# RWKV scan run as two streams half an iteration apart, with three projection groups ahead of the loop

## What is computed

```
n = rmsnorm(h); z = n @ w_in_2            # columns: b, c, h (conv), r, k, v (scan), low ranks
y_conv = b * causal_conv3(c * h)
r, k, v = token_shift(...)                # lerp with the previous position
S_t = S_{t-1} diag(w_t) + (S_{t-1} a_t) b_t^T + v_t k_t^T ;  y_t = S_t r_t      # 16 heads of 64
y = group_norm(y) * ln_x_w + ln_x_b + bonus ; y_rwkv = y * gate
h = h + rmsnorm([y_conv, y_rwkv] @ w_out_2) ; then the feed-forward part
```

## Time and profile before

| | |
|---|---|
| median of 3 runs | 2535.88 us (2532.89 to 2537.92) |
| the profiled execution, its own time | 2540.15 us |
| its span, first to last instruction | 2538.4 us |
| PE busy over the span | 2488.8 us (98%) |
| DVE, ACT, POOL busy | 1660.2, 1209.3, 71.4 us |
| the scan loop (first row of `k1` to first row of `out2`) | 1240.86 to 1670.29 us of the span |

### The profile page before, as it was taken

The page is one execution under the profiler, slowest core; times in us unless marked ns, Lnnn a source line. Parts: engine busy times, 40 slices in busy tenths (PEclk is TensorE's granted clock), DMA queues, the critical chain, the costliest instruction groups (busy, mean ns, idle before and its releaser), DMA issues.

```text
span 2538.4 us, 60881 instructions
## 1 busy us (share of the span) xinstructions
PE 2488.8 (98%) x25657; PEld 2384.6 (94%) x25657; DVE 1660.2 (65%) x2160; ACT 1209.3 (48%) x1447; POOL 71.4 (3%) x74
## 2 busy tenths in 40 slices
PE   8999999999999999999999999999999999999998
PEld 7988999999999999999899988899999999999996
DVE  6776667666666666678765556565766556666666
ACT  5646545554545444456533342345544444444444
POOL 2000000000000000003100000001000000000000
PEclk9999999999999999999999999999999999999999
DMA  6554545655565655655533333345555555555553
GB/s 208 168 148 139 162 151 184 197 184 185 180 188 177 193 181 183 190 179 165 150 106 106 102 106 100 109 136 172 191 184 180 192 188 183 189 183 188 184 181 133
DMA packets 397818, 420.54 MB, mean 166 GB/s; under 512 B 15406, under 2 KB 372498, under 8 KB 397522
## 3 DMA queue, kind: packets, MB, share of 16 engines
q1 hardware_dynamic: 397170, 416.46, 52.8%
q10 hardware_dynamic: 496, 1.84, 0.2%
HBM read 416.14 MB, written 2.10 MB: 165 GB/s over the span
## 4 chain that ended last, share of the span: by engine, by line
PE 93%; DVE 4%; ACT 2%; issue 1%; SPq 0%; DMA 0%; DVEq 0%; ACTq 0%
PE psum L2451 26%; PE psum L2452 25%; PE psum L2453 25%; PE psum L2465 3%; PE psum L2467 3%; PE psum L2466 3%; PE psum L2902 2%; DVE w_lo L1298 1%; ACT w_hi L694 1%; PE psum L3075 1%; PE psum L3032 0%; PE psum L3106 0%; PE psum L3010 0%; PE psum L2679 0%; PE psum L2942 0%
## 5 line engine op out<-in xcount | busy, mean ns | idle before, releaser
L2451 PE MATMUL psum<-act_hi,w_hi 128*128 128x256 f32 (+3 forms) x4736 | 1360.9, 287 | 13.5 <-DVE act_lo L1336 4.3
L2452 PE MATMUL psum<-act_lo,w_hi 128*128 128x256 f32 (+3 forms) x4736 | 1333.3, 282 | 0.0
L2453 PE MATMUL psum<-act_hi,w_lo 128*128 128x256 f32 (+3 forms) x4736 | 1330.2, 281 | 0.3 <-issue 0.3
L694 ACT ACTIVATE w_hi<-raw 128x1024 fp32r<-128x1024 f32 x788 | 830.4, 1058 | 1038.1 <-PE psum L2453 909.0
L1298 DVE TENSOR_TENSOR w_lo<-raw,w_hi 128x1024 fp32r<-128x1024 f32 x788 | 966.3, 1236 | 500.4 <-ACT w_hi L694 499.9
L2451 PEld LDWEIGHTS psum<-act_hi,w_hi 128*128 128x128 f32 x4736 | 892.8, 189 | 29.0 <-DVE act_lo L1336 5.7
L2452 PEld LDWEIGHTS psum<-act_lo,w_hi 128*128 128x128 f32 x4736 | 894.0, 189 | 3.9 <-issue 2.4
L2453 PEld LDWEIGHTS psum<-act_hi,w_lo 128*128 128x128 f32 x4736 | 893.9, 189 | 0.5 <-issue 0.5
L2451 PE MATMUL psum<-ff_hi,w_hi 128*128 128x256 f32 x640 | 181.0, 283 | 4.3 <-DVE up L1317 3.1
L2452 PE MATMUL psum<-ff_lo,w_hi 128*128 128x256 f32 x640 | 179.9, 281 | 0.0
L2453 PE MATMUL psum<-ff_hi,w_lo 128*128 128x256 f32 x640 | 179.8, 281 | 0.0
(11 more groups left out here) (422 smaller groups left out, 1895.9 us busy)
## 6 DMA issues: line engine op xcount, KB each, us to landing
raw<-in_w_in SPq DMA_DIRECT2D x188, 512.0 KB, 3.8
raw<-in_w_up SPq DMA_DIRECT2D x176, 512.0 KB, 3.6
raw<-in_w_down SPq DMA_DIRECT2D x176, 512.0 KB, 4.0
raw<-in_w_gate_up SPq DMA_DIRECT2D x176, 512.0 KB, 3.5
raw<-in_w_out SPq DMA_DIRECT2D x64, 512.0 KB, 3.5
x_rows<-in_x SPq DMA_DIRECT2D x8, 256.0 KB, 5.6
out_x<-out_rows SPq DMA_DIRECT2D x8, 256.0 KB, 2.2
raw<-in_w_in SPq DMA_DIRECT2D x4, 384.0 KB, 3.4
```

The source lines that it names most:

```text
L694: act.activation(w_hi[:, slot], raw[:, slot], ACT.Copy).then_inc(S["hi_done"], 1)
L2451: pe.matmul(out_, wh, xh, start=first and r == 0, stop=False)
L2452: pe.matmul(out_, wh, xl, start=False, stop=False)
L2453: mm = pe.matmul(out_, wl, xh, start=False, stop=last and r == RK - 1)
```

## The change

Iterations now belong to two streams x = 0 and 1: stream 0 takes quarters 0 and 2, stream 1 quarters 1 and 3, six iterations each. Stream 1 runs six stages behind, so that in each slot PE first does a late stage (6 to 11) of one stream and then an early stage (0 to 5) of the other, then the side work, then the rows. There are nine slots ahead of the scan (`PRE`) with 48 rows (groups `k1 r1 v1`), and 78 slots (`STAGES`) in place of 144, with 4 or 3 rows each (short ones at the ends of groups, and none in the last three). The first and third group use bank pair 2, and the first no longer waits for `v0` to leave but for `kk_max`. Evictions of the early stages go through bank 4 in series (ACT waits for DVE's). The bonus sums of quarter 0 move from behind slot 0 into slot 2, the gate of quarter 2 from the loop to behind the first two units of `out2`. The number of small matmuls, rows, evictions and loads stays as it was. A few semaphores are merged, and mask tiles are built elsewhere and then folded.

```
-    SLOTS = 12
-    N_SLOT = 1 + 12 * SLOTS
+    LOOP_IN2 = "k1 r1 v1 k2 r2 v2 b0 k3 r3 v3 c0 h0 b1 c1 h1 b2 c2 h2 b3 c3 h3".split()
+    PRE, SLOTS = 9, 6
+    STAGES = 78
+    N_SLOT = PRE + STAGES
...
+        for n in range(N_SLOT):
+            want += (5, 5, 6)[n % 3] if n < PRE else (4, 4, 4, 4, 3, 4)[(n - PRE) % SLOTS]
+            k = min(min(want, 336) - at, 16 - at % 16)
...
+    def side_pair(n):
+        return 2 if n in (0, 2) else 0
...
+        if q_ == 1:
+            K_SQUARE[1], K_SUM[1], K_CLAMP[1], K_ROOT[1] = at_ + 1, at_ + 2, at_ + 2, at_ + 3
...
@@ VectorE, before the loop
             decay_prev(slice(2, RW))
             lo(u + 20, 0)
+            lo(u + 21, 1)
             k_steps, r_steps = k_finish(0), r_finish(0)
-            for _ in range(4):
+            for _ in range(2):
                 next(k_steps)
-            lo(u + 21, 1)
             leave(u + 20, g0 % 2, heads(Z_V, 0)[:, :, PAD:RT], T2)
             lo(u + 22, 2)
+            for _ in range(2):
+                next(k_steps)
+            lo(u + 23, 3)
...
+            lo(u + 24, 0)
             next(r_steps)
...
-            at_once(v_shift(0))
@@ VectorE, the loop
             def scan_inputs():
+                yield from until(2)
+                yield from v_shift(0)
                 for q in range(1, 4):
...
                 for steps in side:
-                    next(steps, None)
+                    for _ in range(3 if now[0] < PRE else 2):
+                        next(steps, None)
...
+            for _ in range(PRE):
+                serve()
+            for g in range(STAGES):
+                for x in ((1, 0) if g % 12 < 6 else (0, 1)):
+                    if 0 <= g - 6 * x < 72:
+                        stage(x, *divmod(g - 6 * x, 12))
+                serve()
@@ TensorE, side work and rows
+                yield from until(2)
+                bonus_sums(0)
+                for q in range(1, 4):
+                    yield from until(K_SUM[q])
+                    kk_sums(q)
+                    yield from until(BONUS[q])
+                    bonus_sums(q)
...
-                        pe.wait_ge(S["evicted"], gc + n)
+                        if n == 0:
+                            pe.wait_ge(S["kk_max"], 1)
+                        else:
+                            pe.wait_ge(S["evicted"], gc + (n if n > 3 else n - 1))
                     if r == 0:
                         pe.wait_ge(S["lo_done"], uc + 4 * n + j + 1)
@@ TensorE, the loop
+            for _ in range(PRE):
+                fill()
+            for g in range(STAGES):
+                x = g // 6 % 2
+                i, st = divmod(g - 6 * x, 12)
+                j, st_late = divmod(g - 6 * (1 - x), 12)
+                if 0 <= j < 6:
+                    late(1 - x, j, st_late, i)
+                if 0 <= i < 6:
+                    early(x, i, st, j)
+                fill()
```

More of the change, by code:

```diff
@@ L289, in two_blocks, with y_conv @@
     Z_A, Z_R, Z_B, Z_K, Z_V = range(5)
-    y_conv = Z[:, Z_R, :, PAD:RT]
+    def y_conv(first, n):
+        kind = Z_R if first < 4 else Z_K
+        return Z[:, kind, first % 4:first % 4 + n, PAD:RT]
     f_rows = M["mixed"][:].rearrange("p k t -> p (k t)")[:, 0:2 * D] \
@@ L1130, in conv_hi @@
             def conv_hi(tiles):
-                act.activation(act_hi[:, tiles, TC3], y_conv[:, tiles, TC3], ACT.Copy) \
+                y = y_conv(tiles.start, tiles.stop - tiles.start)
+                act.activation(act_hi[:, tiles, TC3], y[:, :, TC3], ACT.Copy) \
                     .then_inc(S["mix_hi"], 1)
@@ L2066, in mask4, with masked @@
                 return over(over(m, 1, 2), 1, 2)
-            def masked(dst, bank, at, mask, part=None):
+            def masked(x, dst, bank, at, mask, part=None):
                 src = psum[0:RB, bank:bank + 2, at:at + 64 if part is None else at + 128]
@@ L2301, in _ @@
                             steps[:, :, AT_Y:AT_Y + 64].rearrange("k c (p t) -> k p c t", p=2)) \
[L2302 to L2303 removed]
+                            .then_inc(S[f"rw_end_{x}"], 1)
+            for _ in range(PRE):
+                serve()
+            for g in range(STAGES):
+                for x in ((1, 0) if g % 12 < 6 else (0, 1)):
+                    if 0 <= g - 6 * x < 72:
+                        stage(x, *divmod(g - 6 * x, 12))
+                serve()
             assert now[0] == N_SLOT
@@ L2950, in side_pe @@
             def side_pe():
-                yield from until(K_SUM[1])
-                kk_sums(1)
-                yield from until(BONUS[1])
-                bonus_sums(1)
-                pe.wait_ge(S["gup_landed"], 16)
+                yield from until(2)
[5 more added lines that the diff above has]
+                    bonus_sums(q)
+                pe.wait_ge(S["low_landed"], 48)
                 for q in range(3):
@@ new lines, in turned, with by_head @@
+            def turned(done, q, tt, kind, bank, at):
+                for p in range(2):
+                    mm = pe.transpose(psum[0:RB, bank, at + P * p:at + P * p + P],
+                                      Z[:, kind, 2 * q + p, RB * tt:RB * tt + RB], ident[:])
+                mm.then_inc(done, 1)
+            def by_head(lhs, rhs, at, wide, start=False, stop=False):
+                for p in range(2):
+                    for c in range(3):
+                        for e in range(2):
+                            o = psum[halfp[e], STEP_BANK + c, at + wide * p:at + wide * p + wide]
+                            mm = pe.matmul(o, lhs(chunk[c], 2 * p + e), rhs(chunk[c], 2 * p + e),
+                                           start=start and p == 0, stop=stop,
+                                           skip_group_check=True)
+                return mm
```

601 lines of the change are left out of this document (301 added, 300 removed).

## The result

The changed kernel takes 2559.47 us (median of 5 runs, 2552.35 to 2565.71) against 2535.88 us of the kernel before (5 runs, 2532.89 to 2539.79): a ratio of 1.0089, 95% interval 1.0066 to 1.0112, so slower by 0.9%. The forecast was 2531.9 us with a range up to 2545. It was wrong in sign and by 27.6 us. Single executions of the changed kernel lie up to 13 us apart.

The account below looks back on a forecast made before the run. PE, busy 98% of the span, bounds the kernel, with at most 14.3 us idle in the loop. -17.2 - 8.6 - 2.5 + 11.7 + 5.6 + 5.5 + 1.5 = -4.0 us: median 2535.88 to 2531.9, range 2521 to 2545.

Parts of the forecast that it names:

- the supply of instructions: PE's fetching of instructions: no term of its own in the sum, let in only as a rival case.
- PE runs out of instructions: Rival: by_head followed at once by l2 in 11 slots, 1.9 us wait each, +17 us, 2549 us; chance 0.09.
- The sign of being wrong that the prediction named: Waits of PE for instructions ("issue") over 6 us in all would show the forecast wrong.
- The clock behind these stops: PE's clock falls after waits of 2 us or more, some 1.4 us each; none charged to instruction waits.
- Fewer visits, -17.2: Loop: 65 fewer visits to small work at 0.31 us, 20.2 at most, 14.1 if shape borders cost; middle taken, -17.2 us.
- Borders of shape: 55 shared slots where tile shape changes between stages: 0.11 us each, 6.1 us, as the bound; the middle was taken.
- Waits taken away, -8.6 and -2.5: Loop start: waits for v0 and k1 gone with their clock, -8.6 us; later groups' waits for the one before, -2.5.
- The lead-in, +11.7: Slots ahead of the scan: new PE waits of 1.7, 4.5, 2.0 and 3.5 us, together +11.7.
- Its clock, forecast at 5.6: Clock falls after the four lead-in waits: 4 x 1.4 = +5.6 us.
- The end, +5.5: Last three slots, without rows: waits of 2.3 and 2.2 us, before one of 0.4, and one clock fall: +5.5 us.
- Inside the loop, +1.5: Five slots with one row after a group's end: serial eviction by DVE and ACT shows for 0.2 to 0.5 us: +1.5.

Follow-up runs that it names:

- Run 1: Changed kernel with two of the slot's rows put between by_head and l2 in the 11 slots that hold both: 2544.37 us, ratio 1.0024 to the kernel before.
- run 9: Changed kernel with two rows between the late and the early stage in every slot that has both: 2567.65 us, ratio 1.0116 to the kernel before.
- runs 1 to 3, 5 to 7, 9 and 10: Changed kernel: by_head split 2544.37 us, lead-in mended 2544.51, end 2559.12; kernel before, extra matmuls: 2573.81, 2558.62; changed kernel: shifted 2564.79, split everywhere 2567.65, split and lead-in 2529.36.
- runs 4, 8, 11 and 12: Changed kernel with by_head split, lead-in and end mended: 2532.90 us; also by_head cut in two: 2534.33; instead shifted by 64 instructions: 2529.35, by 128: 2530.95.

## Why the prediction was wrong

**The step that failed: the supply of instructions stood at nothing in the sum; it took 13.3 us of waits more than before, and the clock behind them.** The prediction names the mechanism among its rivals ("PE runs out of instructions", 2549 us, chance 0.09) and lets it in only there. It argued against it with the mean over the 12 runs of `by_head`, 0.3 us. That mean says nothing of a run that is half as long again. The row to read was the single wait of 1.9 us together with the length of what ran before it: a stretch of small matmuls without rows that fills a block. "`by_head` alone nearly can" swallow a block was misread too: its 288 instructions are more than 256. A block of 256 fits into 288 at 33 of 256 places of the border, into 432 at 177. By that estimate 1.5 of the 12 visits before hold a whole block, and 7.6 of the 11 after; blocks executed in under 2 us were 2 and 9 in the loops. The rival's own figure was 21 us of waits, at 1.9 a visit in 11 slots; measured are 17.5 in 14 places. Its size was near, but it carried no clock. The sign of being wrong that the prediction named, "issue" over 6 us, is the one that came.

**The clock behind these stops: also at nothing.** The forecast charged 1.4 us of clock to each long wait for DVE and forgot it for its instruction rival. Measured, the clock of the loop's inside took some 11.4 us (0.02 x 180 + 0.04 x 196) against 2 before, each known to 2 us. 13.3 + 9.4 = 22.7 us, of the 24.7 that lie between the forecast of -4.0 and the measured +20.7 us of the profiled executions. Run 1 takes 9.7 us of stops out, and the clock of the inside comes back to 0.98 (1300 to 1480 us) and 1.00 (1480 to 1664).

**Fewer visits, -17.2:** right as a number. The rest in the ledger fell by 16.9 us, and run 9, which gives the visits back, puts 11.2 on it again.

**Borders of shape.** At a border where the shape changes the next group starts 0.10 us later than where it doesn't:

```profile
1320.96 0.62 PE L2943 MATMUL psum<-kv_tok,akt 32*32 32x64 f32 x24
1321.51 0.95 PE L3089 MATMUL psum<-z 64*32 64x64 f32 x72
...
1325.75 0.62 PE L2943 MATMUL psum<-b_tok,tt 32*32 32x64 f32 x24
1326.20 0.42 PE L2943 MATMUL psum<-ld,ldt 32*32 32x32 f32 x24
```

Two groups of the same 32x64 operand: 0.55 us to the 64\*32 scores, 0.45 to the 32\*32 `ld`. All 55 borders are like it: the first matmul starts 0.14 to 0.15 us after the last one (one 0.24), against 0.02 to 0.04 at the 11 of equal shape. So the bound of 0.11 for each was right, and not the middle that I took. With it the term is -14.7, and that the ledger has -16.9 all the same is in part luck: the 2 us between them are about what it can't resolve.

**Waits taken away, -8.6 and -2.5:** right. Neither `v0` nor `k1` holds PE up any more, and `gate_c` is down to nothing.

**The lead-in, +11.7:** right in place and near in size, wait by wait:

```profile
1247.34 1.27 PE L2917 MATMUL psum<-bonus,halves 128*128 128x272 f32 x4 [2.35 <-DVE bonus L1998]
...
1263.11 1.33 PE L2905 MATMUL psum<-low,halves 128*128 128x288 f32 x2 [4.92 <-ACT low L1083]
...
1276.90 0.36 PE L2496 MATMUL psum<-act_hi,w_hi 128*128 128x272 f32 x1 [2.02 <-DVE w_lo L1326]
...
1292.11 0.95 PE L3089 MATMUL psum<-z 64*32 64x64 f32 x72 [0.82 <-DVE z L1345]
1295.90 0.39 PE L2496 MATMUL psum<-act_hi,w_hi 128*128 128x272 f32 x1 [2.84 <-DVE w_lo L1326]
```

Forecast 1.7, 4.5, 2.0 and 3.5 in two pieces; measured 2.35, 4.92, 2.02 and 3.66, and 1.6 us in two later waits for `w_lo` that I had not seen: 14.5 in all. Its clock, forecast at 5.6, is 6.9 us (0.11 x 62.6) against 3.6 of the shorter stretch before.

**The end, +5.5:** 3.7 us of waits (4.5 forecast) and 3.4 of clock (0.18 x 19), where one fall of 1.4 was charged. **Inside the loop, +1.5:** 1.2 us in three waits, for `rkt`, `kv_tok` and `low`.

So the terms worked out from durations held to 1 to 3 us each, and what missed was a resource that no row of an engine shows. The ranking of the rivals failed: three points spoke for it (five waits in the rows before, a mechanism with a place, a run made half as long again) and one mean against.

## What to carry to other kernels

Before merging or reordering work on TensorE, look at every "issue" wait of the profile and count the instructions of the short, dense stretch in front of it as the profile has them, weight loads included: if the edit makes such a stretch longer, price a stop of about 4 us (the median here is 3.9, and single ones go to 7) less the time of the last 256 instructions, and some 1.7 us of clock behind it if it is over 1.5 us long, even where the mean over all visits is small. Spread dense small work between long matmuls rather than next to more of it. An edit anywhere ahead also moves the places where these stops fall, so that two edits of a few microseconds need not add up, and one that gains nothing alone may have been masked.

## What the runs showed that I had not expected

**How the clock falls with the length of a stop.** For ten of the kernels (before, after, and runs 1 to 3, 5 to 7, 9 and 10) I took each issue wait of 1300 to 1660 us and the granted clock of the 6 us from its end on. It comes out mostly as 1.00 (2.4 GHz) or about 0.72, that is some 3.4 us at 1.2 GHz, 1.7 us lost.

| wait, us | followed by a clock of 0.73 or less |
|---|---|
| under 0.9 | 0 of 49 |
| 0.9 to 1.2 | 3 of 11 |
| 1.2 to 1.5 | 7 of 16 |
| 1.5 to 2.0 | 13 of 17 |
| 2.0 and more | 18 of 19 |

So the loss isn't proportional: cutting a stop of 2.4 us to 1.0 gives back 1.4 us of waiting and, most often, 1.7 of clock as well. The four kernels left out (runs 4, 8, 11 and 12) agree: 0 of 21, 0 of 8, 1 of 4, 2 of 3, 5 of 6. Run 1 lives on that. Two rows of windows of after, a stop of 2.38 us and one of 1.24:

```profile
1619.36:1625.36 6.00, 6.00 (x114) 5.57 (x115) 3.32 (x9) 1.70 (x5) 0.00 (x0) 0.72 0.04 9
...
1369.90:1375.90 6.00, 6.00 (x102) 5.75 (x103) 3.36 (x7) 2.23 (x4) 0.00 (x0) 1.00 0.33 90
```

**A block of instructions can be late by microseconds at a share of the DMA engines of a third.** Half of the stops have 3.5 to 4.5 us of block and wait together, 18 of 158 have 5 to 7.1. In these 18 the packet was under way for 0.9 to 1.6 us, as elsewhere, but started 2.6 to 4.3 us after the block's first matmul, where the median is 1.4: the lateness lies ahead of the packet. The share of the DMA engines over the loop is 0.36, so that it isn't their total load. Weights moved at 101 GB/s or more in the microsecond before each of the 28 packets that started 2.4 us or later, but at many of the others as well; whether a packet queues behind particular transfers of weights was not tested.
